# A two-block hybrid network on one core: scan steps, latent norms, angles and the modulated norm placed anew

## The chip, the core and the metric

One core of a Trainium2 chip runs the whole program once. The metric is the device time in microseconds of that core, median of the runs.

## The reference, cut to what matters

256 tokens, width 2048, everything in float32. The first block is an S5 layer (a linear state space with a scan over time, gates z and glu) and a forgetting-attention layer. The second block has two hybrid layers, each with retention and latent attention behind a norm that is modulated by a condition vector:

```
xn = rmsnorm(h, g_pre); u, z = split(xn @ w_in)              # S5 layer
y = s5_ssm(u, ...)                                           # h_t = A h_(t-1) + B u_t, y_t = C h_t + D u_t
y = gelu(y); y = y * sigmoid(y @ w_glu + b_glu) * silu(z); h = h + rmsnorm(y @ w_out, g_post)
kvf = rmsnorm(h, g_kv) @ w_kv                                # keys k, values v, forget gates f
...
mod = silu(c) @ w_mod + b_mod; shift, scale, gate = split(mod, 3)          # hybrid layer, twice
h = rms_norm(x, g_norm) * (1 + scale) + shift
rq, rk, rv, rg, cq, ckv, kr, mg, bg = split(h @ w_in)
rq, rk = rope(rq), rope(rk)                                  # cos and sin of positions * frequencies
q = rms_norm(cq, g_cq) @ w_uq; kv = rms_norm(ckv, g_ckv) @ w_ukv; k_rope = rope(kr)
...
```

## The kernel before

Activations lie transposed, features on the 128 partitions and 256 tokens along the free axis, 16 tiles of 256 columns for the width of 2048. Every weight matrix is streamed from memory in blocks of 128 x 2048 floats, one block per output tile, into four buffers `raw`. For precision each operand is split in two halves that TensorE multiplies at full rate: ScalarE rounds a block to `whi` (L512, `split_hi`), VectorE subtracts it to get `wlo` (L1073, `split_lo`), two buffers of each. TensorE multiplies `whi` by both halves of the activations `xs` (L1893) and `wlo` by the high half (L1895); z and a few others take the form at L1888 and L1890, the value projections v and rv the form at L1854.

Each engine has its own instruction list, written out by hand in the order in which it runs; engines meet only at semaphores. `project(key, ..., side=...)` stands in each list for one matrix: for block j it handles output tile j (TensorE multiplies, ScalarE copies one half of the sum to `acctmp`, L560, VectorE adds the other, L1142), then splits block j + 2, then calls `side(j)`, the place where everything else is hung in. So VectorE's order in block j is: a multiply-add of the modulation stream if the matrix has one (L1101, `modacc`), the sum of tile j, the split of block j + 2, side(j). With `held` the last split of a matrix is left out and issued later by hand. SyncE loads a `raw` buffer again as soon as `w_lo_done` says that its block is split. TensorE may start a tile once the tile two before it has been summed (`acc_summed`).

The places that the change touches:

- z (first block, 16 tiles): `scan_step` runs the S5 scan beside z on VectorE, 62 steps of four instructions (L1267, `s5c` and `ring`); `scanned_by[j]` says how many steps are done after side(j). ScalarE copies the states to `state` in groups of four (`keep_states`, L736), in a ring of twelve. Then TensorE computes the state outputs (`carried`, L2089), which wait for all the states.
- v: `trig_side` on VectorE takes the angles from the positions (`reduce_angle`, L1256 to L1264), seven or eight instructions that each wait for the one before, in blocks 4, 6, 8 and 10; block 13 scales two groups of the next norm (`norm_split`, L1217). The values' tiles are finished only in every fourth block (3, 7, 11, 15), two at a time, and summed at L1134. ScalarE takes the sines in blocks 8 and 12 (L858).
- the modulated norm (`modulate` on ScalarE, L612 and L631; `norm_modulated` on VectorE): four groups of four tiles. VectorE multiplies a group by the reciprocal root (L1267, `stg`), ScalarE applies scale and shift in four instructions (L612), copies the high half (L631), VectorE subtracts for the low half (L1205). The first tile of rq waits for one group after the other.
- the latent norms: cq (512 features) is normalised beside ckv, and ckv beside mg, in one side call each (`latent`): root, reciprocal (L1192), four scalings (L1217), high half (L631), low half (L1205). `mg_side(2)` on VectorE rotates the rope keys.
- `ret_side(0)` on TensorE, beside ga: the wait before the retention scores (L2178), for the last rotation (`rope_done`) and for the centred values (`values_centred`, ScalarE, L547).

## Time and profile before

| | |
|---|---|
| median of 3 runs | 3175.7 us (3175.69 to 3175.76) |
| profiled execution | 3178.53 us |
| its span | 3176.8 us |
| mean granted TensorE clock | 0.986 of full speed |
| TensorE (PE) | busy 95% of the span |
| VectorE (DVE) | 68% |
| ScalarE (ACT) | 48% |
| the 16 DMA engines | mean 203 GB/s |

The span runs from the first to the last instruction of the profiled execution; its own time has 1.7 us more around it. Busy shares are means over stages with different limits. The list of waits gives, for each pair of line and releaser, the idle time of the engine before that line. A matmul counts as busy until its modelled end.

### The profile page before, as it was taken

The page shows a single profiled execution, that of the slowest core. Times are in us where ns is not written, and L with a number is a line of the kernel's source. Part 1 is how long each engine was busy: PE and PEld are TensorE (multiplying, and loading weights), DVE is VectorE, ACT ScalarE, POOL GpSimd, SP SyncE. Part 2 cuts the span into 40 slices and gives each one's busy share as a digit, 9 for nine tenths or more (in the row PEclk, how much of TensorE's full clock was granted, in tenths as well). Part 3 has the DMA queues.
Part 4 walks back from the last instruction along what each step waited for, and adds up shares of the span by engine and source line. Part 5 has one row for each costly group of instructions (what it writes and reads, how often), then busy time and mean ns, then how long its engine had stood idle before and what let it go on. Part 6 is the DMA issues. An engine that isn't in the chain of part 4 may idle for free.

```text
span 3176.8 us, 50173 instructions
## 1 busy us (share of the span) xinstructions
PE 3025.8 (95%) x20326; PEld 2634.6 (83%) x20326; DVE 2154.8 (68%) x2512; ACT 1537.5 (48%) x2007; POOL 108.0 (3%) x206
## 2 busy tenths in 40 slices
PE   6998998999999799999999999989999999999998
PEld 5898887877888687888888888878788888888887
DVE  7688777877865657667765667764755776655565
ACT  5454455334445546345455444453534544554444
POOL 0000000000000000000000000000000000000000
PEclk9999998999999999999999999999999999999999
DMA  5334675776544457656654477645754566445543
GB/s 220 121 108 147 212 257 218 278 257 233 206 166 169 164 200 275 239 189 235 236 215 146 173 283 264 230 182 200 260 191 171 200 234 230 145 174 211 186 176 129
DMA packets 103460, 645.73 MB, mean 203 GB/s; under 512 B 11616, under 2 KB 12640, under 8 KB 40160
## 3 DMA queue, kind: packets, MB, share of 16 engines
q1 hardware_dynamic: 71568, 508.12, 45.1%
q0 software_dynamic: 28528, 105.92, 9.3%
q10 hardware_dynamic: 3168, 28.84, 2.3%
q8 instruction: 152, 2.49, 0.3%
q14 instruction: 44, 0.36, 0.0%
HBM read 628.15 MB, written 14.68 MB: 202 GB/s over the span
## 4 chain that ended last, share of the span: by engine, by line
PE 78%; DVE 12%; ACT 6%; issue 2%; DMA 1%; DVEq 0%; ACTq 0%; POOLq 0%
PE acc L1893 39%; PE acc L1895 19%; PE acc L1854 8%; DVE wlo L1073 4%; PE acc L1888 3%; ACT whi L512 3%; DVE xs L1205 1%; PE acc L1890 1%; DVE s5c L1267 1%; PE bank L2038 1%; DVE w L1267 1%; DVE stg L1726 1%; DVE modacc L1101 1%; PE bank L2233 1%; DMA modw<-in_modstream 1%
## 5 line engine op out<-in xcount | busy, mean ns | idle before, releaser
L1893 PE MATMUL acc<-xs,whi 128*128 128x512 f32 x6192 | 2211.7, 402 | 71.6 <-DVE xs L1205 52.2
L1895 PE MATMUL acc<-xs,wlo 128*128 128x256 f32 x6192 | 1743.0, 281 | 0.0
L1893 PEld LDWEIGHTS acc<-xs,whi 128*128 128x128 f32 x6192 | 1170.6, 189 | 366.7 <-issue 36.4
L1073 DVE TENSOR_TENSOR wlo<-raw,whi 128x2048 fp32r<-128x2048 f32 x451 | 1033.6, 2292 | 505.0 <-ACT whi L512 504.1
L1895 PEld LDWEIGHTS acc<-xs,wlo 128*128 128x128 f32 x6192 | 1177.8, 190 | 1.3 <-issue 0.6
L512 ACT ACTIVATE whi<-raw 128x2048 fp32r<-128x2048 f32 x451 | 860.2, 1907 | 111.9 <-PE acc L1854 105.2
L560 ACT ACTIVATE acctmp<-acc 128x256 f32<-128x256 f32 x387 | 148.0, 383 | 987.6 <-PE acc L1895 976.8
L1142 DVE TENSOR_TENSOR w<-acc,acctmp 128x256 f32<-128x256 f32 (+1 forms) x352 | 152.3, 433 | 328.9 <-ACT acctmp L560 328.2
L1854 PE MATMUL acc<-whi,xs 128*128 128x512 f32 x768 | 242.7, 395 | 11.9 <-DVE w L1134 7.1
L1101 DVE SCALAR_TENSOR_TENSOR modacc<-modw,cact,modacc 128x1024 f32<-128x1024 f32 x180 | 230.2, 1279 | 6.9 <-DMA modw<-in_modstream 6.5
L1854 PEld LDWEIGHTS acc<-whi,xs 128*128 128x128 f32 x768 | 145.7, 190 | 46.7 <-issue 8.3
L491 POOL DMA_DIRECT2D modw<-in_modstream x192 | 101.5, 529 | 2225.7 <-DVE modacc L1098 1254.2
L1854 PE MATMUL acc<-wlo,xs 128*128 128x512 f32 x384 | 151.0, 393 | 0.0
L650 ACT ACTIVATE smx<-smx,stat 128x128 f32<-128x128 f32 x96 | 43.0, 448 | 170.4 <-DVE stat L1293 170.4
L1086 DVE TENSOR_TENSOR wlo<-raw,whi 128x512 fp32r<-128x512 f32 (+1 forms) x96 | 74.7, 780 | 61.3 <-ACT whi L519 60.1
L1888 PE MATMUL acc<-xs,whi 128*128 128x256 f32 x512 | 94.5, 287 | 2.2 <-DVE wlo L1073 2.2
L1854 PEld LDWEIGHTS acc<-wlo,xs 128*128 128x128 f32 x384 | 73.0, 190 | 14.8
L1888 PEld LDWEIGHTS acc<-xs,whi 128*128 128x128 f32 x512 | 81.0, 195 | 2.5 <-DVE wlo L1073 2.4
L1888 PE MATMUL acc<-cqs,whi 128*128 128x256 f32 x384 | 71.5, 288 | 2.5 <-DVE wlo L1086 1.1
L1890 PE MATMUL acc<-xs,wlo 128*128 128x256 f32 x256 | 73.2, 286 | 0.0
L519 ACT ACTIVATE whi<-raw 128x512 fp32r<-128x512 f32 (+1 forms) x96 | 66.7, 695 | 0.2
L1888 PEld LDWEIGHTS acc<-cqs,whi 128*128 128x128 f32 x384 | 59.6, 192 | 4.6 <-DVE wlo L1086 1.9
(304 smaller groups left out, 2313.9 us busy)
## 6 DMA issues: line engine op xcount, KB each, us to landing
raw<-in_wstream SPq DMA_DIRECT2D x479, 1024.0 KB, 4.8
modw<-in_modstream POOLq DMA_DIRECT2D x192, 512.0 KB, 4.6
residual<-h ACTq DMA_DIRECT2D x2, 2048.0 KB, 10.9
ga_gate<-w ACTq DMA_DIRECT2D x2, 2048.0 KB, 10.5
gated_retention<-w ACTq DMA_DIRECT2D x2, 2048.0 KB, 7.9
h<-gated_retention ACTq DMA_DIRECT2D x2, 2048.0 KB, 10.2
h<-residual ACTq DMA_DIRECT2D x2, 2048.0 KB, 9.4
ga_w<-ga_gate ACTq DMA_DIRECT2D x8, 512.0 KB, 10.1
```

What stands on the lines that cost most here:

```text
L491: pool.dma_start(modw[s][:, :], src).then_inc(mod_loaded[s], 16)
L512: act.activation(whi[s % SPL][:, :], raw[slot][:, :], ACT.Copy).then_inc(w_hi_done, 1)
L560: act.activation(acctmp[:, par % 2, :], acc[par % 2][:, T:2 * T], ACT.Copy, scale=FOX_SCALE if key == (None, "q") else 1.0).then_inc(acc_l ...
L1073: dve.tensor_tensor(out=wlo[s % SPL][:, :], in0=raw[s % RAW][:, :], in1=whi[s % SPL][:, :].bitcast(F32), op=ALU.subtract).then_inc(w_lo_do ...
L1086: ins = dve.tensor_tensor(out=wlo[n % SPL][:, c], in0=raw[n % RAW][:, c], in1=whi[n % SPL][:, c].bitcast(F32), op=ALU.subtract)
L1101: dve.scalar_tensor_tensor(out=modacc[:, :], in0=modw[s % 2][:, :], scalar=scale, in1=modacc[:, :], op0=ALU.mult, op1=ALU.add).then_inc(mo ...
L1142: dve.tensor_tensor(out=dest(jt), in0=turn(acc[par % 2][0:rows, 0:T]), in1=turn(acctmp[0:rows, par % 2, :]), op=ALU.add).then_inc(acc_summ ...
L1854: mm = pe.matmul(acc[t % 2][:, :], x_split[:, k0 + k, a, tokens], part_w[:, c], start=(first and k == 0 and part_w is whi[w] and a == 0), ...
L1888: pe.matmul(acc[par % 2][:, 0:T], whi[w][:, c:c + cols], x_split[:, k, a, :], start=(k == 0 and a == 0), stop=False, skip_group_check=True)
L1890: mm = pe.matmul(acc[par % 2][:, 0:T], wlo[w][:, c:c + cols], x_split[:, k, 0, :], start=False, stop=(k == kts - 1), skip_group_check=True)
L1893: pe.matmul(acc[par % 2][0:cols, :], whi[w][:, c:c + cols], x_split[:, k, :, :], start=(k == 0), stop=False, skip_group_check=True)
L1895: mm = pe.matmul(acc[par % 2][0:cols, 0:T], wlo[w][:, c:c + cols], x_split[:, k, 0, :], start=False, stop=(k == kts - 1), skip_group_check ...
```

## The change

- `scanned_by` puts two scan steps fewer into block 4 of z and stays two behind until block 13; block 14 gets five. z's last two weight splits (`held=2`) leave the loop on VectorE and are issued behind the last scan step. VectorE no longer waits for the end of each z tile.
- The two latent norms are cut over two blocks: root and reciprocal in one, scalings and halves in the next. The key rotation moves from mg's block 2 to block 4.
- The angles are computed in `angle_step`, three instructions a block from block 2 to block 12 of v; positions are converted in block 1. The eight scalings of the next norm go two a block into blocks 11 to 14. The second pair of sines moves to block 13.
- In groups 1 and 3 of the modulated norm VectorE multiplies by the modulated scale and the reciprocal root at once (four instructions), ScalarE adds the shift while it writes the high half, and VectorE adds the shift again while it subtracts (four instructions).
- TensorE waits for `values_centred` in block 2 of ga instead of block 0, and for the sums of rv in block 0.

```diff
@@ -121,6 +121,7 @@
 MID_KNOWN = 6
+SHIFT_LATE = (1, 3)
 FOX_FIRST = 3
@@ -424,7 +425,7 @@
-        scanned_by = (4, 12, 20, 28, 36, 37, 38, 39, 42, 45, 48, 51, 54, 57, 60, 62)
+        scanned_by = (4, 12, 20, 28, 34, 35, 36, 37, 40, 43, 46, 49, 52, 55, 60, 62)
@@ -607,6 +608,15 @@
                     act.wait_ge(sem("norm_scaled"), 4 * (name == "pre_l1") + g + 1)
+                    if g in SHIFT_LATE:
+                        act.wait_ge(acc_done, JOBS[(0 if name == "pre_l0" else 1, "rq")][1])
+                        for k in range(4):
+                            i = 4 * g + k
+                            last = act.activation(xs[:, i, 0, :], stg_half(g)[:, k, :], ACT.Identity, bias=mv[:, i:i + 1])
+                            if k == 2:
+                                last.then_inc(x_staged, 1)
+                        last.then_inc(x_hi_done, 1)
+                        continue
                     for k in range(4):
@@ -852,8 +862,8 @@
-                if j in (8, 12):
-                    kind = (j - 8) // 4
+                if j in (8, 13):
+                    kind = (j - 8) // 5
                     act.wait_ge(sem("trig_arg"), kind + 1)
@@ -983,6 +993,7 @@
                         root(f"cq{l}")
+                    if j == 3:
                         act.wait_ge(sem("residual_away"), 16 * (l + 1))
@@ -994,8 +1005,8 @@
                         root(f"ckv{l}")
+                    if j == 2:
                         split_x(f"ckv{l}", lambda g: ckr[:, :, :], cks, 0)
-                    if j == 2:
                         act.wait_ge(acc_summed, JOBS[(l, "mg")][1])
@@ -1122,9 +1133,6 @@
                             lo_piece(*piece, q)
-                        if key == (None, "z"):
-                            dve.wait_ge(acc_done, t + 1)
-                            continue
                         if one_half(key, jt) or key[1] == "rv":
@@ -1144,7 +1152,7 @@
                             link(tt(dest(jt), dest(jt), rstd[0:rows, :], ALU.mult))
-                    if whole and split_ahead(key, j) and not (held and j == JOBS[key][2] - 1):
+                    if whole and split_ahead(key, j) and not (held and isinstance(j, int) and j >= JOBS[key][2] - held):
                         split_lo(j + (b0 + SPL), b0 + s + SPL)
@@ -1230,10 +1238,25 @@
                             dve.wait_ge(x_lo_done, SPLIT_BEFORE[name] + g - 1)
-                        tt(stg_half(g), group(src)(g), bcast(spread_rstd(name), 4), ALU.mult).then_inc(sem("norm_scaled"), 1)
+                        if g in SHIFT_LATE:
+                            for k in range(4):
+                                i = 4 * g + k
+                                ins = dve.scalar_tensor_tensor(out=stg_half(g)[:, k, :], in0=src[:, i, :], scalar=gsc[:, i:i + 1],
+                                                               in1=spread_rstd(name), op0=ALU.mult, op1=ALU.mult)
+                            ins.then_inc(sem("norm_scaled"), 1)
+                        else:
+                            tt(stg_half(g), group(src)(g), bcast(spread_rstd(name), 4), ALU.mult).then_inc(sem("norm_scaled"), 1)
                     if g == 3:
                         split_held((0, "out") if l else (None, "foxout"))
-                    if g >= 1:
+                    if g - 1 in SHIFT_LATE:
+                        dve.wait_ge(x_hi_done, SPLIT_BEFORE[name] + g)
+                        for k in range(4):
+                            i = 4 * (g - 1) + k
+                            ins = dve.scalar_tensor_tensor(out=xs[:, i, 1, :], in0=stg_half(g - 1)[:, k, :],
+                                                           scalar=modv[l][:, i:i + 1], in1=xs[:, i, 0, :].bitcast(F32),
+                                                           op0=ALU.add, op1=ALU.subtract)
+                        ins.then_inc(x_lo_done, 1)
+                    elif g >= 1:
                         split_x(name, stg_half, xs, g - 1)
@@ -1476,7 +1499,9 @@
                     output_power(3, (j - 5,))
-            project((None, "z"), None, side=z_side)
+            project((None, "z"), None, side=z_side, held=2)
+            split_lo(GLU_BLOCK, GLU_BLOCK)
+            split_lo(GLU_BLOCK + 1, GLU_BLOCK + 1)
             dve.wait_ge(sem("c_sigmoid"), 1)
@@ -1582,20 +1607,50 @@
+            def angle_step(n):
+
+                kind, n = divmod(n, 16)
+                quarter, n = (0, n) if n < 8 else (1, n - 7)
+                angle, k, dst = angs[1][:, :], angs[2][:, :], trig[:, kind, 1 - quarter, :]
+                if n == 0:
+                    link(dve.tensor_scalar(angle, angs[0][:, :], invf[:, kind:kind + 1], None, ALU.mult))
+                if n == 1:
+                    link(dve.tensor_scalar(k, angle, 1 / (2 * math.pi), 0.25 * quarter, ALU.mult, ALU.add))
+                if n == 2:
+                    link(dve.tensor_scalar(k, k, MAGIC, None, ALU.add))
+                if n == 3:
+                    link(dve.tensor_scalar(k, k, MAGIC, None, ALU.subtract))
+                if n in (4, 5, 6):
+                    link(dve.scalar_tensor_tensor(out=dst, in0=k, scalar=-(TWO_PI_1, TWO_PI_2, TWO_PI_3)[n - 4],
+                                                  in1=angle if n == 4 else dst, op0=ALU.mult, op1=ALU.add))
+                if n == 7 and quarter:
+                    link(dve.tensor_scalar(dst, dst, math.pi / 2, None, ALU.add))
+                if n == 7 + quarter:
+                    ins = dve.tensor_scalar(dst, dst, PI, -PI, ALU.min, ALU.max)
+                    if quarter:
+                        ins.then_inc(sem("trig_arg"), 1)
+
+            def pre1_tile(i):
+
+                return dve.scalar_tensor_tensor(out=stg_half(i // 4)[:, i % 4, :], in0=h[:, i, :], scalar=vcol("norm_pre1")(i),
+                                                in1=rstd[:, :], op0=ALU.mult, op1=ALU.mult)
+
             def trig_side(j):
-                if j == 3:
+                if j == 1:
                     dve.wait_ge(sem("positions_loaded"), 16)
                     link(dve.tensor_copy(angs[0][:, :], posi[:, :]))
-                if j in (4, 8):
-                    kind = (j - 4) // 4
-                    link(dve.tensor_scalar(angs[1][:, :], angs[0][:, :], invf[:, kind:kind + 1], None, ALU.mult))
-                    link(reduce_angle(trig[:, kind, 1, :], angs[1][:, :], angs[2][:, :], False))
-                if j in (6, 10):
-                    kind = (j - 6) // 4
-                    reduce_angle(trig[:, kind, 0, :], angs[1][:, :], angs[2][:, :], True).then_inc(sem("trig_arg"), 1)
-                if j == 13:
-                    norm_split("pre1", h, vcol("norm_pre1"), stage_only=True)
+                for n in range(3 * (j - 2), 3 * (j - 1)):
+                    if 0 <= n < 32:
+                        angle_step(n)
+                if j in (11, 12):
+                    for i in range(2 * j - 18, 2 * j - 16):
+                        pre1_tile(i)
+                if j in (13, 14):
+                    for i in range(2 * j - 26, 2 * j - 24):
+                        last = pre1_tile(i)
+                    if j == 14:
+                        last.then_inc(x_staged, 2)
             project((None, "v"), lambda j: tile(w2, j), side=trig_side)
@@ -1732,15 +1787,22 @@
                 def latent(n, lat, dst):
-                    rms(f"{n}{l}")
                     norm_split(f"{n}{l}", lat, vcol(f"g_{n}{l}"), staged=lambda g: lat[:, :, :], dst=dst)
-                project((l, "ckv"), lambda j: tile(ckr, j), side=lambda j: latent("cq", cqr, cqs) if j == 2 else None)
+
+                def cq_side(j):
+                    if j == 2:
+                        rms(f"cq{l}")
+                    if j == 3:
+                        latent("cq", cqr, cqs)
+                project((l, "ckv"), lambda j: tile(ckr, j), side=cq_side)
                 project((l, "kr"), lambda j: krope[:, :])
                     if j == 1:
+                        rms(f"ckv{l}")
+                    if j == 2:
                         latent("ckv", ckr, cks)
-                    if j == 2:
+                    if j == 4:
                         link(rope(ROPE_L * l + 8, rtmp[:, 0:1, :], krope[:, :].rearrange("p (a t) -> p a t", a=1), 1, 1))
@@ -2194,6 +2256,8 @@
                         pe.wait_ge(rope_done, ROPE_L * l + 8)
+                        pe.wait_ge(acc_summed, JOBS[(l, "ga")][1])
+                    if j == 2:
                         pe.wait_ge(sem("values_centred"), RET_H * (l + 1))
```

## Rows read from the trace of the kernel before

**Rows 1.** Page, first section: busy time (share of the span) and instructions.

```profile
PE 3025.8 (95%) x20326; PEld 2634.6 (83%) x20326; DVE 2154.8 (68%) x2512; ACT 1537.5 (48%) x2007; POOL 108.0 (3%) x206
```

**Rows 2.** Waits of TensorE: line <- releaser: us in total, times, longest.

```profile
PE acc L1893 <- DVE xs L1205: 52.2, 18, 8.7
...
PE acc L1854 <- DVE w L1134: 7.1, 3, 3.2
```

**Rows 3.** Timeline, TensorE: start, us, instruction, [idle before <- releaser], four stretches.

```profile
244.36 0.51 PE L1888 MATMUL acc<-xs,whi 128*128 128x256 f32 x2 [2.19 <-DVE wlo L1073]
...
305.35 4.92 PE L2089 MATMUL bank<-vall,state 64*64 64x64 f32 x87 [7.42 <-ACT state L736]
...
1273.10 0.70 PE L2178 MATMUL bank<-w 128*128 128x256 f32 x2 [1.52 <-DVE w L1267]
...
1523.74 0.50 PE L1893 MATMUL acc<-xs,whi 128*128 128x512 f32 x1 [1.61 <-DVE wlo L1073]
...
1550.27 0.50 PE L1893 MATMUL acc<-xs,whi 128*128 128x512 f32 x1 [2.14 <-DVE wlo L1073]
```

**Rows 4.** Windows: length, PE, PEld, DVE, ACT, POOL busy, PEclk, DMA share, GB/s.

```profile
244.40:248.70 4.30, 4.30 (x24) 4.30 (x25) 4.27 (x6) 0.93 (x1) 0.00 (x0) 0.61 0.74 244
248.70:251.80 3.10, 3.10 (x27) 3.10 (x27) 3.07 (x6) 0.00 (x0) 0.00 (x0) 0.99 0.35 42
305.30:310.20 4.90, 4.85 (x91) 4.88 (x93) 0.00 (x0) 0.00 (x0) 0.00 (x0) 0.50 0.33 135
310.20:316.00 5.80, 5.80 (x203) 5.80 (x199) 2.14 (x4) 1.99 (x4) 0.00 (x0) 1.00 0.01 3
657.00:659.60 2.60, 2.04 (x10) 1.36 (x9) 2.49 (x4) 0.52 (x2) 0.00 (x0) 1.00 0.65 197
685.20:689.00 3.80, 3.80 (x10) 3.06 (x11) 3.58 (x3) 0.00 (x0) 0.53 (x1) 0.56 0.88 259
1523.70:1529.50 5.80, 5.76 (x33) 5.01 (x33) 3.28 (x3) 0.65 (x1) 0.53 (x1) 1.00 0.74 256
```

**Rows 5.** Timeline, VectorE beside z: splits (wlo) and the scan's last instruction.

```profile
242.02 2.28 DVE L1073 TENSOR_TENSOR wlo<-raw,whi 128x2048 fp32r<-128x2048 f32 x1
...
254.21 2.29 DVE L1073 TENSOR_TENSOR wlo<-raw,whi 128x2048 fp32r<-128x2048 f32 x1 [1.04 <-ACT whi L512]
...
294.51 2.29 DVE L1073 TENSOR_TENSOR wlo<-raw,whi 128x2048 fp32r<-128x2048 f32 x1
...
300.26 2.29 DVE L1073 TENSOR_TENSOR wlo<-raw,whi 128x2048 fp32r<-128x2048 f32 x1
...
304.41 0.29 DVE L1267 TENSOR_TENSOR ring<-s5c 128x128 f32<-128x128 f32 x1
```

**Rows 6.** Timeline, VectorE beside v, blocks 6 and 7.

```profile
680.42 0.29 DVE L1256 TENSOR_SCALAR angs<-angs 128x256 f32<-128x256 f32 x1
...
681.40 0.43 DVE L1259 SCALAR_TENSOR_TENSOR trig<-angs,angs 128x256 f32<-128x256 f32 x1
...
683.32 1.28 DVE L1101 SCALAR_TENSOR_TENSOR modacc<-modw,cact,modacc 128x1024 f32<-128x1024 f32 x1
684.51 0.87 DVE L1134 TENSOR_SCALAR w<-acc,ms 128x256 f32<-128x256 f32 x2
```

**Rows 7.** Timeline, VectorE and ScalarE in the latent norms of the first layer.

```profile
1514.67 1.75 DVE L1192 RECIPROCAL rstd<-rstd 128x256 f32<-128x256 f32 x1 [0.48 <-ACT rstd L620]
1516.46 1.67 DVE L1217 SCALAR_TENSOR_TENSOR cqr<-cqr,vec,rstd 128x256 f32<-128x256 f32 x4
1519.32 1.23 DVE L1205 TENSOR_TENSOR cqs<-cqr,cqs 128x1024 fp32r<-128x1024 f32 x1 [1.19 <-ACT cqs L631]
...
1544.17 1.06 ACT L631 ACTIVATE cks<-ckr 128x1024 fp32r<-128x1024 f32 x1 [3.53 <-DVE ckr L1217]
```

**Rows 8.** Timeline, VectorE in the modulated norm of the first layer.

```profile
1078.64 1.22 DVE L1267 TENSOR_TENSOR stg<-h,rstd 128x1024 f32<-128x1024 f32 x1
1080.49 1.23 DVE L1205 TENSOR_TENSOR xs<-stg,xs 128x1024 fp32r<-128x1024 f32 x1 [0.64 <-ACT xs L631]
...
1086.73 1.23 DVE L1205 TENSOR_TENSOR xs<-stg,xs 128x1024 fp32r<-128x1024 f32 x1 [0.42 <-ACT xs L631]
```

## The prediction

> **What bounds the kernel now.** I read the page's first section, then the list of TensorE's waits, then the rows just behind each wait. TensorE is busy for 95% of the span [rows 1], so an edit on another engine is worth something only where TensorE stands still, or runs at the lower of its two clocks after standing still. Of the waits the change can reach [rows 2], the reader is to see four places. (a) The scan beside z: TensorE stands 2.19 us before the eighth tile of z, and 7.42 us between z and the state outputs [rows 3]. (b) The value projection v: three waits for VectorE's sum of a tile, 7.1 us together, the longest 3.2 [rows 2]; in the trace they are 0.6, 3.25 and 3.25. (c) The latent norms: 1.61 and 2.14 us before two weight splits [rows 3], and the same pair 1050.6 us later in the second layer, so four waits. (d) The modulated norm at the head of each layer, most of the 52.2 us behind L1205 [rows 2]. For the fifth edit (e) the wait is 1.52 us at L2178 [rows 3], also twice.
>
> **(a) Scan ahead of the splits.** VectorE has no pause here: one split and three scan steps fill 5.75 us, 294.51 to 300.26 [rows 5]; less 2.29 for the split, a step is 1.15 us. The new table puts six steps instead of eight behind block 4, and keeps two steps of lag from there to block 13. So the split that TensorE waited for at 244.36 begins 2 x 1.15 = 2.3 us before 242.02 and is done at 242.0, when TensorE's tile before it ends (244.36 - 2.19 = 242.17). The 2.19 us go. So does the slow stretch behind them: 24 matmuls took 4.3 us at a granted clock of 0.61, where the next 27 took 3.1 us at 0.99 [rows 4]; 4.3 - 24 x 0.115 = 1.5 us. TensorE is 3.7 to 3.9 us earlier from there on. VectorE is earlier by 2.3 us plus the 1.04 it used to wait for ScalarE at 254.21 [rows 5], 3.4 in all, so each later split, which used to be done about 1.0 us before TensorE wanted it (288.7 + 2.3 against 292.0), keeps some 0.5 us. That is thin, but the period of 5.75 doesn't exceed z's 48 matmuls x 0.12 = 5.76.
> The tail: the scan's last step ended at 304.41 + 0.29 = 304.70 [rows 5]. Now, from 294.51 - 3.4 = 291.1, come five steps (5.8) and two (2.3) with no split between: 299.15. The states' copy and TensorE follow as before, at 299.8 instead of 305.35: **-5.5 us**. This includes the 3.8 above, since the later start is what counts. The wait for the end of each z tile that VectorE loses is implied by ScalarE's half of the split; the ring of states keeps its copies (step 57 wants twelve groups, copied beside block 12). The two splits moved behind the scan (299.2 to 303.8) are covered by the state outputs: VectorE idled from 304.8 to 311.6 before, and 306.1 answers to that end now; without this cover they would cost 4.6. SyncE's load of the fifth glu block waits for the first of them, 5 us later than now, against a use after 345: nothing. The state outputs start at the lower clock, 91 matmuls in 4.9 us against 203 in the next 5.8 [rows 4]. The idle time before them shrinks from 7.4 to some 5.8 us, so how long the low clock lasts is not given by a row: at most 91 x (53.8 - 28.6 ns) = 2.3 us gained, and as much lost if it lasted twice as long. I take 0.6, near no change: **-0.6 us**.
>
> **(b) Angles spread, first norm groups in four pieces.** Eight operations in one block (680.42 to 683.32, 2.90 us) made VectorE late for the multiply-add of the modulation (1.19) and with it for the sum that frees TensorE's accumulator [rows 6]. A TENSOR_SCALAR with its wait takes 0.33, a fused one 0.46. Before the sum of block 7 now stand two fused and one plain, 1.25: the wait of 3.25 becomes 1.6. Before block 11's, three plain ones, 0.98: 3.25 becomes 1.33. Before block 3's, three at 1.04 where none was: 0.58 becomes 1.62. Together 1.65 + 1.92 - 1.04 = 2.5 us. After each long wait TensorE ran at a clock of 0.56 to 0.58: 10 matmuls in 3.8 us against 10 in about 2.1 [rows 4], 1.5 us, twice: 3.0. The wait of 1.61 us at 1523.74 is followed by a granted clock of 1.00 [rows 4], so I take the whole 3.0; nothing to 3.0 is the range. Pieces of the norm (0.42 a piece, four of them 1.67 [rows 7]) leave block 13 with 0.8 instead of 3.3 us and bring the last multiply-add 0.3 us forward. In every other block VectorE has 2.2 + 1.2 + 1.1 to 2.2 against 5.44 of TensorE, so these steps are hidden; that cover is 0.9 us and more. Positions are used two blocks earlier, at 652.4, 12 us after they landed: nothing. **-5.8 us**.
>
> **(c) Latent norms in two blocks.** Before, reciprocal (1.75), four scalings (1.67), ScalarE's half (1.06) and the difference (1.22) all stood before the next split [rows 7]. With the scalings a block later, VectorE splits mg's first block at 1518.9 to 1521.1; TensorE starts it at 1522.0 instead of 1523.74, -1.75. What is late next is ScalarE: it waits for the scalings (1522.75), makes its half, and only then copies kr and splits the next block, which VectorE finishes at 1528.3, 0.6 us after TensorE wants it. Net -1.15. For ckv: the split is done at 1547.1, before it is wanted at 1548.1, so -2.14; but ScalarE waits for the scalings until 1548.8, then half (1.06), swap (0.85), copy, split, and VectorE is done at 1555.1 where TensorE wants it at 1553.7: +1.4. With the queue's 0.15, net -0.9. The keys' rotation, two blocks later, falls into a block with 0.8 us to spare. Two layers: **-4.1 us**; if the new waits are absent -7.5, if they are half as long again -2.
>
> **(d) Modulated scale by VectorE in groups 1 and 3.** ScalarE paced this pipeline: VectorE waited 0.64 and 0.42 us for it [rows 8]. ScalarE loses two halves of 1.06. VectorE's product of 1.22 becomes four fused operations, 1.67, and its difference likewise. Between the first difference and the last it gains three times 0.45 = 1.35 and loses 1.06 of waiting; the split held for the layer stands among them and moves too. End of the last difference +0.35, and the last quarter of TensorE's first tile with it. Two layers: **+0.7 us**; -0.5 to +1.5.
>
> **(e) The values' wait.** TensorE's wait of 1.52 us ends with VectorE's L1267 [rows 3], the last rotation, whose wait stays where it is. The centring was over 6 us before. The added wait is for sums already made. **0**, at most 0.2 either way.
>
> **The sum** is -5.5 - 0.6 - 5.8 - 4.1 + 0.7 = -15.3 us on the profiled execution's 3178.5 (span 3176.8); the runs' median lies 2.8 us below that execution, and the same difference gives 3175.7 - 15.3 = **3160.4**.
>
> **Rule against row.** The rows show the clock at its lower level, 1.2 instead of 2.4 GHz, after TensorE stood for 2.19 and 3.25 us [rows 3, 4]. The Trainium skill, page "TensorE: Matmul & The Clock Gate", section "HAM oscillation — how this bites in real kernels", counts only idle gaps longer than each of these as a danger. By that rule none of the three slow stretches should be there, and removing the gaps would return only their own length: 4.5 us less, 3164.9. The row differs and decides.
>
> **The rivals.** (1) *The clock stays as expensive*: the three remaining waits in v (1.3 to 1.6 us) are each followed by the lower clock. For it: after 2.19 us it fell. Against: after 1.61 it didn't [rows 4]. Then v gives -1.3 at best and the whole -10.8: 3164.9. Chance 0.10. (2) *New waits take the places*: VectorE misses z's splits, whose margin is 0.5 us, and the two latent waits are as long as those removed. Then (a) gives -3, (c) 0, the sum -8.1: 3167.6. Chance 0.07. (3) *The norm gives more*: DMA and clock fall better behind the earlier start (waits of 2.2 to 2.9 us at the heads of later stages sometimes carry the low clock, 1.5 us each), two or three of them: 3156.5. Chance 0.13. (4) *Within 0.2%*: TensorE is earlier, but the modulation's stream makes the q stage and the s5out stage wait as long again, so that only half arrives: 3170. Chance 0.05. (5) *Slower*: steps spread one to three a block cost what their waits cost, not their length. It decides once a step in v takes over 0.3 us more than the 0.33 to 0.46 of the row, since then every block overruns 5.44; at 1.3 us more a step ten blocks pay 3.0 each, +30 us, giving 3190. Against it, the same operations stand back to back with the same waits in rows 6. Chance 0.03. (6) *An edit doesn't do what it says* (e, or d): both are near 0 in the sum already.
>
> **How the numbers follow.** My forecast 3160.4 has 0.62. The range of 8 in 10 must take in rivals 1 and 3 and the bounds of (b), (c) and the clock in (a): 3155.0 to 3167.0. About 0.2% (6.3 us) is what a measurement can tell from no change: below 3169.4 is faster, 0.92; 0.05 the same; 0.03 slower.
>
> **What the new profile would show.** No wait of L1888 in z; state outputs at 299.8 +- 0.7; two splits behind the last scan step. In v, waits near 1.6, 1.6 and 1.3 and no clock below 1.00. In both layers, waits at mg's blocks 1 and 5 instead of 0 and 4. VectorE without pause in the modulated norm. L2178's wait unchanged. It would be wrong if z's splits are late, or if the latents' waits only move.

## The result, and the profile after

The changed kernel takes 3159.7 us, the median of 9 executions (3153.2 to 3169.5). Nine executions of the kernel before, on the same chip, have a median of 3173.9 (3163.1 to 3182.1). The ratio is 0.995, 95% interval 0.9938 to 0.9962: of 3173.9 us that is 15.9 us less (12.1 to 19.7). The prediction was 15.3 less, 3160.4. The profiled execution of the changed kernel took 3157.37 us, with a span of 3155.7 and a mean granted clock of 0.987, against 3176.8 and 0.986.

Those two traces differ by 21 us, more than the medians do. Single executions of one kernel scatter by about 10 us on either side, and the 21 us lie outside the interval of the medians, so the 5 us surplus is not put down to the change; part of the work below is to find where it sits.

The page of the changed kernel, first section, answers to [rows 1] (busy time, share of the span, instructions):

```profile
PE 3017.1 (96%) x20326; PEld 2627.1 (83%) x20326; DVE 2157.7 (68%) x2536; ACT 1532.7 (49%) x2003; POOL 108.5 (3%) x206
```

Its waits of TensorE, answering to [rows 2] (line <- releaser: us in total, times, longest). L1955 is now what L1893 was, L1916 what L1854 was:

```profile
PE acc L1955 <- DVE xs L1213: 49.6, 18, 8.7
PE acc L1955 <- DVE wlo L1084: 15.7, 23, 2.5
...
PE bank L2151 <- ACT state L746: 5.3, 1, 5.3
...
PE acc L1916 <- DVE w L1142: 5.0, 3, 1.8
```

The waits of v are 5.0 us instead of 7.1, the wait of z before its eighth tile is gone (no line L1950 with a weight split of 2.2 us), and the one before the state outputs is 5.3 instead of 7.4. The timeline of TensorE in the changed kernel shows each in its place, answering to [rows 3]:

```profile
298.36 1.94 PE L2151 MATMUL bank<-vall,state 64*64 64x64 f32 x31 [5.28 <-ACT state L746]
...
653.15 0.47 PE L1916 MATMUL acc<-whi,xs 128*128 128x512 f32 x1 [1.62 <-DVE w L1142]
677.02 0.47 PE L1916 MATMUL acc<-whi,xs 128*128 128x512 f32 x1 [1.83 <-DVE w L1142]
700.60 0.47 PE L1916 MATMUL acc<-whi,xs 128*128 128x512 f32 x1 [1.56 <-DVE w L1142]
...
1260.66 0.70 PE L2240 MATMUL bank<-w 128*128 128x256 f32 x2 [1.52 <-DVE w L1290]
...
1516.27 0.50 PE L1955 MATMUL acc<-xs,whi 128*128 128x512 f32 x1 [0.65 <-DVE wlo L1084]
1542.16 0.49 PE L1955 MATMUL acc<-xs,whi 128*128 128x512 f32 x1 [1.39 <-DVE wlo L1084]
```

Windows of the changed kernel, answering to [rows 4] (the clock is the number before the DMA share):

```profile
298.30:304.40 6.10, 6.04 (x114) 6.07 (x116) 3.89 (x3) 0.00 (x0) 0.00 (x0) 0.50 0.58 192
304.40:310.20 5.80, 5.80 (x185) 5.73 (x183) 2.81 (x4) 2.53 (x4) 0.00 (x0) 1.00 0.41 168
...
677.00:684.00 7.00, 6.98 (x31) 5.82 (x32) 4.61 (x6) 1.75 (x2) 1.06 (x2) 1.00 0.81 291
```

VectorE at the scan's end: its last step, and the two splits that now stand behind it, answering to [rows 5]:

```profile
297.41 0.29 DVE L1290 TENSOR_TENSOR ring<-s5c 128x128 f32<-128x128 f32 x1
297.62 4.49 DVE L1084 TENSOR_TENSOR wlo<-raw,whi 128x2048 fp32r<-128x2048 f32 x2
```

And VectorE in the modulated norm of the first layer, answering to [rows 8]:

```profile
1059.16 1.23 DVE L1290 TENSOR_TENSOR stg<-h,rstd 128x1024 f32<-128x1024 f32 x1
1060.30 1.67 DVE L1244 SCALAR_TENSOR_TENSOR stg<-h,gsc,rstd 128x256 f32<-128x256 f32 x4
1063.67 1.23 DVE L1213 TENSOR_TENSOR xs<-stg,xs 128x1024 fp32r<-128x1024 f32 x1 [1.71 <-ACT xs L641]
...
1066.08 1.67 DVE L1255 SCALAR_TENSOR_TENSOR xs<-stg,modv,xs 128x256 fp32r<-128x256 f32 x4
...
1072.70 1.67 DVE L1255 SCALAR_TENSOR_TENSOR xs<-stg,modv,xs 128x256 fp32r<-128x256 f32 x4
1077.90 0.42 DVE L1150 TENSOR_TENSOR w<-acc,acctmp 128x256 f32 x1 [3.54 <-ACT acctmp L561]
```

The pauses of 0.64 and 0.42 between the differences are gone, as predicted; the wait before the first difference, 2.15 us before, is still 1.71. The last row is the first sum of rq: it comes 3.53 us after the last difference, where it came 2.39 after it before.

### The profile page after: what moved, and what is told of

Same layout as the page of the kernel before. It is cut to its first block, busy times and chain, and to the rows that moved or that the text cites. A ratio compares the mean times of both kernels' runs of the same rounds, so it can differ in the third digit from the quotient of the medians.

```text
span 3155.7 us, 50181 instructions
## 1 busy us (share of the span) xinstructions
PE 3017.1 (96%) x20326; PEld 2627.1 (83%) x20326; DVE 2157.7 (68%) x2536; ACT 1532.7 (49%) x2003; POOL 108.5 (3%) x206
## 4 chain that ended last, share of the span: by engine, by line
PE 80%; DVE 11%; ACT 6%; issue 2%; DMA 0%; DVEq 0%; ACTq 0%; POOLq 0%
PE acc L1955 39%; PE acc L1957 20%; PE acc L1916 8%; DVE wlo L1084 4%; PE acc L1950 3%; ACT whi L513 3%; DVE xs L1213 2%; PE acc L1952 2%; PE bank L2100 1%; DVE w L1290 1%; DVE stg L1781 1%; PE bank L2297 1%; PE bank L2112 1%; PE bank L2151 1%; PE bank L2298 1%
## 5 line engine op out<-in xcount | busy, mean ns | idle before, releaser
L1955 PE MATMUL acc<-xs,whi 128*128 128x512 f32 x6192 | 2208.0, 401 | 65.6 <-DVE xs L1213 49.6
L1955 PEld LDWEIGHTS acc<-xs,whi 128*128 128x128 f32 x6192 | 1168.4, 189 | 361.1 <-issue 36.6
L1916 PE MATMUL acc<-whi,xs 128*128 128x512 f32 x768 | 239.6, 391 | 9.8 <-DVE w L1142 5.0
L1916 PEld LDWEIGHTS acc<-whi,xs 128*128 128x128 f32 x768 | 144.2, 188 | 43.4 <-DVE wlo L1084 7.4
L1916 PE MATMUL acc<-wlo,xs 128*128 128x512 f32 x384 | 149.5, 389 | 0.0
L1950 PE MATMUL acc<-xs,whi 128*128 128x256 f32 x512 | 92.9, 284 | 0.0
L1916 PEld LDWEIGHTS acc<-wlo,xs 128*128 128x128 f32 x384 | 72.1, 188 | 14.7
L1950 PEld LDWEIGHTS acc<-xs,whi 128*128 128x128 f32 x512 | 79.7, 192 | 0.1
L1950 PE MATMUL acc<-cqs,whi 128*128 128x256 f32 x384 | 71.4, 287 | 2.6 <-DVE wlo L1097 1.1
L1950 PEld LDWEIGHTS acc<-cqs,whi 128*128 128x128 f32 x384 | 59.5, 191 | 4.6 <-DVE wlo L1097 1.9
```

The source lines that it names most:

```text
L1916: mm = pe.matmul(acc[t % 2][:, :], x_split[:, k0 + k, a, tokens], part_w[:, c], start=(first and k == 0 and part_w is whi[w] and a == 0), ...
L1950: pe.matmul(acc[par % 2][:, 0:T], whi[w][:, c:c + cols], x_split[:, k, a, :], start=(k == 0 and a == 0), stop=False, skip_group_check=True)
L1955: pe.matmul(acc[par % 2][0:cols, :], whi[w][:, c:c + cols], x_split[:, k, :, :], start=(k == 0), stop=False, skip_group_check=True)
```

## The experiments

**How they are compared.** Every kernel has the same 20326 matmuls in the same order. So the start of the same matmul can be looked up in two traces, and the difference over a stretch is what the stretch gained. The limits are times of the kernel before; positive is us gained against its trace. z is 186 to 300, v 640 to 737, the latents 1500 to 1560 and 2550 to 2611, the modulated norms 1040 to 1090 and 2110 to 2145.

| kernel | z | v | latents 1 | latents 2 | mod. norm 1 | mod. norm 2 | all the rest | whole trace |
|---|---|---|---|---|---|---|---|---|
| changed | 6.02 | 6.05 | 1.78 | 1.48 | -2.80 | -0.58 | 9.08 | 21.03 |
| (a) alone | 5.97 | 0.36 | -0.01 | -0.02 | -0.21 | -1.19 | 5.88 | 10.78 |
| (b) alone | -0.13 | 4.47 | -1.34 | -0.22 | -3.20 | -0.70 | 4.14 | 3.02 |
| (c) alone | 1.50 | 0.30 | 1.78 | 1.45 | -0.12 | -1.35 | 15.53 | 19.09 |
| (d) alone | -0.02 | -1.17 | -1.54 | -0.02 | -3.88 | -1.06 | 2.65 | -5.04 |
| (e) alone | 1.42 | 0.28 | -1.39 | -1.41 | -0.27 | -0.61 | 10.94 | 8.96 |
| all three follow-ups | 5.97 | 9.34 | 4.25 | 4.46 | -0.57 | 1.55 | 8.38 | 33.38 |

The column of the rest is the warning: no part touches what is in it, and it runs from 2.7 to 15.5 here, and from -1.9 to 15.5 over all the kernels of this document.

### One part at a time

Four kernels: the kernel before with the hunks of one part of the diff each, as the prediction names them. Of (a), beside the lines that let `project` hold two splits:

```diff
-        scanned_by = (4, 12, 20, 28, 36, 37, 38, 39, 42, 45, 48, 51, 54, 57, 60, 62)
+        scanned_by = (4, 12, 20, 28, 34, 35, 36, 37, 40, 43, 46, 49, 52, 55, 60, 62)
...
-                        if key == (None, "z"):
-                            dve.wait_ge(acc_done, t + 1)
-                            continue
...
-            project((None, "z"), None, side=z_side)
+            project((None, "z"), None, side=z_side, held=2)
+            split_lo(GLU_BLOCK, GLU_BLOCK)
+            split_lo(GLU_BLOCK + 1, GLU_BLOCK + 1)
```

> Only the scan's new table and z's two held splits on VectorE; the rest is the kernel before. My theory (the prediction's part a): the 2.19 us wait in z and its slow stretch go, the state outputs start 5.5 us earlier than in the kernel before, and about 5 us of time go in all, ratio 0.9982 to 0.9986. Rival, new waits take the places: TensorE waits for z's splits in several tiles and the state outputs start 3 us earlier or less, ratio 0.999 and more.

Measured: 3169.5 us against 3174.4, ratio 0.9985 (0.9972 to 0.9997), which is in the range expected. In the trace z gained 5.97.

(b), the `angle_step` and `trig_side` hunks and ScalarE's sines in block 13:

> Only the angles three steps a block and the norm's pieces in v. My theory: v's waits are 1.6, 1.6 to 1.8 and 1.3 to 1.6 us instead of 0.6, 3.25, 3.25, the granted clock stays at its upper level through v, and v is 5.8 us shorter, half of it from the clock. Rival, the clock stays as expensive: each of the three waits is followed by a stretch at the lower level of 1.5 us cost, and v is only 1.3 us shorter. Ratio 0.9980 by the first, 0.9996 by the second.

Measured: 3174.9 against 3174.4, ratio 0.9999 (0.9985 to 1.0013). The waits are those of the changed kernel, but v gained 4.47 instead of 6.05. The timeline of TensorE, and two windows behind the second wait:

```profile
683.50 0.47 PE L1884 MATMUL acc<-whi,xs 128*128 128x512 f32 x1 [1.83 <-DVE w L1134]
```

```profile
683.60:687.80 4.20, 4.20 (x12) 3.30 (x13) 3.86 (x6) 0.38 (x1) 0.53 (x1) 0.59 0.88 269
687.80:692.00 4.20, 4.20 (x20) 3.46 (x20) 0.62 (x1) 1.18 (x1) 0.53 (x1) 1.00 0.85 343
```

The same wait of 1.83 us that left the clock at 1.00 in the changed kernel is followed here by 0.59: 12 matmuls where the next 4.2 us hold 20. The 1.6 us between 6.05 and 4.47 are this stretch: up to the matmul of 685.2 us the two gained the same (0.61 and 0.63), at 691 us 2.23 and 0.66. For the whole kernel the run is inconclusive: its interval reaches from 4.8 us less to 4.1 more, which just holds the local gain.

(c), `cq_side`, `latent`, the two `split_x` on ScalarE and the key rotation:

> Only the latent norms over two blocks and the key rotation two blocks later. My theory: in each layer TensorE waits 0.6 us before mg's second block and 1.4 us before its sixth instead of 1.6 before the first and 2.1 before the fifth, 2.0 us a layer, 4.1 in all, ratio 0.9987. Rival, the waits only move: their sum stays 3.7 us a layer, ratio 1.000.

Measured: 3165.6 against 3174.4, ratio 0.9981 (0.9968 to 0.9994). The waits of 0.65 and 1.39 are there, at 1520.42 and 1546.32; the latents gained 1.78 and 1.45, 3.2 in all. The interval of the ratio is 1.9 to 10.2 us less.

(d), `modulate` and `norm_modulated`:

> Only the modulated norm with VectorE's scale in two groups. My theory: VectorE is the bound, and from the first difference (L1205 of before) to the end of the last it takes 10.6 to 10.9 us as before (10.58 in the first layer, 10.87 in the second), so the time is within 0.7 us, ratio 1.0000 to 1.0002. Rival, it costs the clock: TensorE runs at the lower level behind its second wait in that tile, as in the changed kernel, because the change makes it so; then the first tile of rq ends 1.2 us later in each layer, 2.4 in all, ratio 1.0008. If the lower clock there doesn't show in this run, it isn't this edit that brings it.

Measured: 3175.4 against 3174.4, ratio 0.9998 (0.9987 to 1.001). Its trace does show the lower clock in the first tile of rq; whether the edit brings it is taken up below, with all traces.

The four ratios add up to 0.37%, 11.7 us, against 15.9 (12.1 to 19.7) for the whole. With intervals of 4 us each way on every part that is agreement, no more.

### Which half of (a) does it

Two kernels: the held splits with the old table, and the new table without the held splits.

```diff
-                        if key == (None, "z"):
-                            dve.wait_ge(acc_done, t + 1)
-                            continue
...
+            project((None, "z"), None, side=z_side, held=2)
+            split_lo(GLU_BLOCK, GLU_BLOCK)
+            split_lo(GLU_BLOCK + 1, GLU_BLOCK + 1)
```

VectorE's wait for the end of each z tile goes with this half. In the kernel before VectorE stood for no such end between 195 and 304 us, so the splits are what this kernel tests.

> The kernel before with one half of part (a): z's last two weight splits are issued behind the last scan step, the table of scan steps stays as it was. My theory (two effects that add: the table starts z's eighth tile earlier, the held splits end the scan earlier): the wait of 2.19 us before z's eighth tile stays, the last scan step ends two splits (4.6 us) earlier, and the state outputs start near 301.0 us, 4.4 us earlier than before. The rival (the table alone does it, because the splits only hide behind ScalarE's copies of the states): state outputs at 304 to 305 us, at most 1 us gained.

```diff
+        scanned_by = (4, 12, 20, 28, 34, 35, 36, 37, 40, 43, 46, 49, 52, 55, 60, 62)
```

> The other half of part (a): the new table of scan steps alone; the last two splits stay in the loop. My theory: no wait before z's eighth tile and no low clock behind it, so TensorE is 3.8 us earlier inside z, but stands that much longer at z's end, since the scan still ends behind both splits: state outputs near 304.4 us, about 1 us gained. The rival: the state outputs come as much earlier as z does, near 301.5 us.

Their whole times, 3174.4 and 3172.3 against 3173.1, are single executions and say nothing. All traces have a first product of the output powers early in z (L2050 before), and the times of the table are counted from its start. That is 193.88 us in the kernel before:

```profile
193.88 1.30 PE L2050 MATMUL bank<-w,k 128*128 128x256 f32 x7 [0.71 <-ACT k L729]
```

| kernel | idle before z's eighth tile, clock behind it | scan's last step ends | state outputs start |
|---|---|---|---|
| before | 2.19, 0.61 | +110.82 | +111.47 |
| (e) alone, z as before | 2.15, 1.00 | +109.30 | +109.95 |
| new table alone | none | +109.19 | +109.84 |
| held splits alone | 2.07, 1.00 | +104.79 | +106.18 |
| (a) alone | none | +104.81 | +105.47 |
| changed | none | +104.79 | +105.45 |

The kernel with (e) alone has z as it was, and it makes the table readable. Windows of 4.3 us just behind that wait, of the kernel with (e) alone (for the kernel before it is the first of [rows 4]):

```profile
243.10:247.40 4.30, 4.24 (x35) 4.24 (x36) 4.27 (x7) 1.04 (x1) 0.00 (x0) 1.00 0.62 242
```

35 matmuls instead of 24 behind a wait of the same length. So the low clock there is no fixed price: of six kernels that keep this wait, it followed in three (waits of 2.19, 2.20, 2.21) and did not in three (2.07, 2.15, 2.16). Where it didn't, the scan ended 1.5 us earlier with nothing changed. VectorE shows the way: its wait of 1.04 us for ScalarE before a split in z ([rows 5]) stands in the three traces with the low clock there and in none of the other eleven. From the trace without it the held splits give 109.30 - 104.79 = 4.5 us, two splits, and the new table 0.1 at the scan's end. What the table adds is at the state outputs: with the splits held but the old table they start 1.39 us after the scan's last step, released by ScalarE's copy of the states, with both 0.66 us after it. These are 0.7 us: at the state outputs the held splits alone are worth 109.95 - 106.18 = 3.8 us, with the table 4.5. Why the copy is late with the old table was not looked into. Otherwise the table only takes away the wait that may bring the low clock. The theory of two effects that add was half right: the held splits gave what was expected of them (within 0.7 us), and the 3.8 us earlier tiles inside z gave nothing, as expected of the table alone.

### Without (d), and (e) alone

> The changed kernel without part (d), so with the modulated norm as it was. If (d) is worth next to nothing, as the trace of it alone says: VectorE's stretch from the first difference to the last one takes 10.6 us in layer 1 and 10.9 in layer 2, with its pauses of 0.64 and 0.42 us back, and the first tile of rq is summed as soon after the last difference as the clock allows, 2.4 to 3.7 us; the rest of the program is as in the changed kernel, span 3155 to 3160 us. The rival, that (d) brings 1.5 to 3 us where the modulated norm runs (the changed kernel is 2.8 us shorter between 1040 and 1090 us): here that stretch is as long as in the kernel before.

Measured: 3158.0 us, one execution, beside 3157.4 for the profiled one of the changed kernel; the two pauses are back (0.63 and 0.41 us). The expectation has a sign wrong: between 1040 and 1090 us the changed kernel is 2.8 us longer than the kernel before, not shorter. Here that stretch is 0.4 us longer. (b) alone, which has no (d) either, is 3.2 us longer there, so this pair decides nothing. (e) alone:

```diff
                         pe.wait_ge(rope_done, ROPE_L * l + 8)
+                        pe.wait_ge(acc_summed, JOBS[(l, "ga")][1])
+                    if j == 2:
                         pe.wait_ge(sem("values_centred"), RET_H * (l + 1))
```

> The kernel before with part (e) alone: TensorE waits for the centred values in ga's third block and for the sums of rv in the first. Predicted nothing: the wait before the retention scores stays 1.52 us in both layers, and stays named after VectorE's last rotation. It is also as good as a second trace of the kernel before. If the low clock falls at other waits from one execution to the next, the stretches around 957 to 1090, 1840 and 2110 to 2140 us differ from the trace of before by 1.5 to 4 us though nothing there is changed; if the clock is set by the program alone, they agree within 0.3 us.

Measured: 3169.4 us against 3173.1, single executions. The wait stays, here in both layers:

```profile
1264.27 0.70 PE L2178 MATMUL bank<-w 128*128 128x256 f32 x2 [1.51 <-DVE w L1267]
...
2313.32 0.70 PE L2178 MATMUL bank<-w 128*128 128x256 f32 x2 [1.52 <-DVE w L1267]
```

So (e) is worth nothing, and this trace, 9.0 us shorter than that of the kernel before, shows what two executions of as good as one program differ by: 1.42 in z, 1.4 the other way in each layer's latents (the low clock behind another spot), and the remainder in stretches that nobody touched. Of the stretches that the expectation named none differs as much as it said: 957 to 1090 gained 0.4 us in all, 1820 to 1860 gained 0.1, 2110 to 2140 lost 0.3. The differences of its size lie elsewhere (2.1 us at 1890 to 1920, beside those in z and in the latents). They decide against a clock set by the program alone. One pair of rows shows it best, the wait before mg's fifth block in the first layer, 2.14 us in both traces. The kernel before:

```profile
1550.27 0.50 PE L1893 MATMUL acc<-xs,whi 128*128 128x512 f32 x1 [2.14 <-DVE wlo L1073]
...
1550.30:1554.60 4.30, 4.30 (x24) 3.74 (x25) 4.20 (x8) 2.28 (x3) 0.53 (x1) 1.00 0.91 316
```

and the one with (e) alone:

```profile
1541.71 0.52 PE L1893 MATMUL acc<-xs,whi 128*128 128x512 f32 x1 [2.14 <-DVE wlo L1073]
...
1541.70:1546.00 4.30, 4.29 (x15) 3.71 (x16) 4.20 (x8) 2.28 (x3) 0.53 (x1) 0.60 0.86 301
```

24 matmuls against 15 behind a wait of one length, so the length of the wait does not decide it.

For the modulated norm I take two lengths: from the start of VectorE's first multiplication by the reciprocal root to the end of its last difference, and to the start of the first sum of rq.

| kernel | layer 1: last difference | first sum | layer 2: last difference | first sum |
|---|---|---|---|---|
| before | 15.09 | 17.48 | 15.38 | 17.77 |
| changed without (d) | 15.09 | 17.48 | 15.39 | 19.03 |
| changed | 15.21 | 18.74 | 15.19 | 18.92 |
| (d) alone | 15.21 | 19.83 | 15.19 | 18.83 |
| follow-up: latents in three blocks, with (d) | 15.20 | 17.60 | 15.18 | 18.77 |
| follow-up: held split late, with (d) | 13.74 | 16.12 | 13.71 | 16.11 |

VectorE's own time is the same to 0.2 us with and without (d). What varies is the 2.4, 3.6 or 4.6 us behind it: TensorE has one more piece of the norm to multiply, at the full or at the low clock, after standing 1.7 to 3.2 us for it. In layer 2 the longer end came in 11 of 12 traces with this wait, whether (d) was in or not. In layer 1 it came in 1 of 8 without (d) and in 3 of 4 with it. That hints that (d) costs a share of 1.1 to 2.2 us in layer 1, but with so few traces it stays open; the ratio of (d) alone bounds it, between 3.2 us more and 4.1 less for all of (d).

### Follow-ups: taking the remaining waits away

All three start from the changed kernel. First, the latent norms over three blocks:

```diff
                     if j == 3:
-                        latent("cq", cqr, cqs)
+                        scale_latent("cq", cqr)
...
+                    if j == 0:
+                        split_x(f"cq{l}", lambda g: cqr[:, :, :], cqs, 0)
+                    if j == 3:
+                        scale_latent("ckv", ckr)
+                    if j == 5:
+                        split_x(f"ckv{l}", lambda g: ckr[:, :, :], cks, 0)
```

> The changed kernel with the latent norms cut over three blocks: reciprocal, scalings, and halves and difference each in a block of its own, and the key rotation one block on. My theory of the two new waits (0.65 us before mg's second block and 1.39 before its sixth: ScalarE must wait for the scalings before it makes its half, and so copies and splits late): ScalarE finds the scalings done a block before, both waits go, and nothing of the same size comes in their place, so 2.0 us a layer more than the changed kernel, 4.1 in all, in the stretches 1500 to 1560 us and its like 1045 us later. The rival (the waits come from VectorE's own work, which is 0.4 to 0.7 us too much for two blocks however it is cut): the waits stay within 0.5 us of 2.04 in sum, or move one block on.

Measured: 3153.9 us, one execution. The waits before mg's second and sixth block are gone in both layers, and nothing stands in their place. One window over both spots, the changed kernel and this one:

```profile
1515.00:1545.00 30.00, 27.96 (x156) 23.90 (x155) 23.86 (x24) 16.45 (x17) 2.12 (x4) 1.00 0.66 226
```

```profile
1515.00:1545.00 30.00, 30.00 (x173) 26.36 (x172) 24.33 (x23) 16.42 (x17) 2.64 (x5) 1.00 0.72 249
```

TensorE is busy for 30.00 of 30 us instead of 27.96: the 2.04 us. The stretches gained 4.84 and 4.04 against the kernel before, so 3.1 and 2.6 more than the changed kernel. Of these 2.4 a layer fall at the two waits: each cost TensorE 0.16 to 0.18 us more than its length in the changed kernel. The others are spread over stretches without any wait (the two paces of the last section). Who was late is read from ScalarE, in the changed kernel:

```profile
1535.64 1.06 ACT L641 ACTIVATE cks<-ckr 128x1024 fp32r<-128x1024 f32 x1 [3.94 <-DVE ckr L1225]
```

and in this one:

```profile
1541.83 1.05 ACT L641 ACTIVATE cks<-ckr 128x1024 fp32r<-128x1024 f32 x1
```

It stood 3.94 us for the scalings, with the copy of a tile and the next weight block queued behind; now they are done when it comes.

Second, the angle steps four a block in eight blocks, with no step in the blocks just ahead of the sums of the values' tiles (2, 6, 10):

```diff
-                for n in range(3 * (j - 2), 3 * (j - 1)):
-                    if 0 <= n < 32:
+                beside = (3, 4, 5, 7, 8, 9, 11, 12)
+                if j in beside:
+                    for n in range(4 * beside.index(j), 4 * beside.index(j) + 4):
                         angle_step(n)
```

> The changed kernel with the angle steps placed four a block in blocks 3, 4, 5, 7, 8, 9, 11 and 12 of v, so that none but the modulation's multiply-add stands right before a sum of a tile of values... except that block's own work. My theory: what TensorE waits for in v is the length of the steps between a tile's end and its sum, each 0.33 to 0.46 us; with none there, the waits of 1.62, 1.83 and 1.57 us go back to about 0.6 each, which is 3.0 us less for v than in the changed kernel, and no low clock. The rival (the waits are the multiply-add's and would be the same without the steps): they stay above 1.3 us, and v takes as long.

Measured: 3155.5 us, one execution. All three waits are at 0.57 to 0.58, and v gained 9.33 instead of 6.05, 3.3 us more:

```profile
652.82 0.47 PE L1917 MATMUL acc<-whi,xs 128*128 128x512 f32 x1 [0.57 <-DVE w L1142]
675.42 0.47 PE L1917 MATMUL acc<-whi,xs 128*128 128x512 f32 x1 [0.58 <-DVE w L1142]
698.05 0.47 PE L1917 MATMUL acc<-whi,xs 128*128 128x512 f32 x1 [0.58 <-DVE w L1142]
```

Third, the held weight split behind the last difference:

```diff
-                    if g == 3:
-                        split_held((0, "out") if l else (None, "foxout"))
...
+                split_held((0, "out") if l else (None, "foxout"))
```

> The changed kernel with the held weight split (2.1 us of VectorE) issued behind the last difference of the modulated norm instead of between the differences. VectorE has no pause there in the changed kernel, so its own work is what sets the last difference: my theory is that the time from the first multiplication to the end of the last difference shrinks from 15.2 us by 1.2 to 2.1 us in each layer (ScalarE's halves bound it from below), and that TensorE's first tile of rq is summed as much earlier, less or more 1.2 us by the clock. The rival (ScalarE or the clock sets the end): it shrinks by less than 0.5 us, or TensorE waits for the split behind it instead, and rq's first tiles are done at the same time.

Measured: 3164.3 us, one execution, whose trace lost 3.2 us before 186 and 3.5 between 300 and 440, where nothing differs; the norm is read from the table above. VectorE is done 1.5 us earlier, and both layers' first sums come 2.4 us behind the last difference: the wait before the tile's last piece is now 1.2 and 1.0 us, and the low clock followed it in neither layer of this kernel, nor of the one with all three. TensorE of this kernel:

```profile
1075.81 0.50 PE L1954 MATMUL acc<-xs,whi 128*128 128x512 f32 x1 [1.18 <-DVE xs L1213]
1078.03 0.49 PE L1954 MATMUL acc<-xs,whi 128*128 128x512 f32 x1 [0.54 <-DVE xs L1253]
1080.23 0.50 PE L1954 MATMUL acc<-xs,whi 128*128 128x512 f32 x1 [0.54 <-DVE wlo L1084]
```

The last row is the split that was moved: TensorE waits 0.54 us for it, so the rival was right about a part. The second sum of rq comes 22.6 us after the first multiplication, in the changed kernel 24.4, in the kernel with the latents in three blocks (no low clock in layer 1) 23.3: 0.7 us by the move itself and 1.1 by the clock.

Then all three together:

> All three at once on the changed kernel: latent norms over three blocks (4 us), angle steps off the sums (3 us), held split late (2 us). If the waits that I name are each the last thing late in their stage, the sum is 9 us less than the changed kernel: about 3151 us, a ratio to the kernel before of 0.992. If the waits only move, it stays at 3158 to 3160, a ratio of 0.995.

Measured: **3145.4 us** (3141.1 to 3148.6, 6 executions) against 3172.7 (11 executions), ratio **0.9915** (0.9901 to 0.9929), and the interval does not touch that of the changed kernel. By the rows it should be 13.1 us below the changed kernel: 3.3 in v, 5.4 in the latents (8.71 - 3.26), and in the modulated norms 2.6 + 2.8 to the first sum (its own are 16.13 and 16.11) less twice the 0.54 of the new wait. The medians differ by 14.2 us, the ratios by 0.35%, 11.1 us. The expectation had said 9: it gave the latents 4 and the late split 2, and left out what the lower clock costs in the modulated norm. Its waits of TensorE:

```profile
PE acc L1964 <- DVE xs L1215: 47.1, 18, 8.7
...
PE acc L1964 <- DVE wlo L1086: 11.1, 20, 1.5
```

## Why the prediction was right

The sum of 15.3 us stands against 15.9 measured (12.1 to 19.7), and the range and the side were right. Its terms were not all so.

**(a), predicted -5.5 and -0.6.** The state outputs came 6.02 us earlier on the trace's own count, so -5.5 was 0.5 short. In the prediction's own sum the 2.3 us of the table come back as two more steps in block 14, so its -5.5 is two splits, 4.6, and VectorE's 1.04 us of waiting for ScalarE. The first is right: the runs give 4.5, and the table moves the scan's end by 0.1 us. The second is no fixed price: it comes with the low clock behind the wait of 2.19, which followed in three of six traces, and together they hold the scan back 1.5 us. So over executions (a) is worth some 5.3 us, not 6.0: 4.5 plus half of 1.5. The low clock in the state outputs, where 0.6 was to be gained, went the other way: it lasted from 298.3 to 304.4, 6.0 us of the work instead of 4.9, and by the matmul that started at 316 us the gain of 6.02 is 5.49, so 0.5 lost. In the text both ends of this term had been kept, 2.3 gained and 2.3 lost.

**(b), predicted -5.8; the trace 6.05.** The waits were foretold as 1.62, 1.6 and 1.33, and are 1.62, 1.83 and 1.56. The steps before the sums of blocks 7 and 11 took the 1.25 and 0.98 us of the prediction (from 673.95 to 675.20, and from 697.79 to 698.77). What was off is the base that they stand on: the prediction took 2.90 us of steps off a wait of 3.25, which leaves 0.35, but with no step there the wait is 0.58, as the second follow-up shows. 0.58 + 1.25 is 1.83 and 0.58 + 0.98 is 1.56: of the 2.90 in the kernel before 0.23 had been hidden. The waits therefore gave 2.07 us and not 2.5. Other terms made up for it: behind each of the two long waits 1.6 us of clock came back (3.2, not 3.0; the prediction's own rows, 3.8 against 2.1, say 1.7), and ahead of the second and third wait TensorE was 0.23 us earlier each time. The 0.3 us of the last multiply-add was not kept: 0.34 us appears at the matmul of 737 us and is given back by that of 745, so v is worth 5.71 in this trace. Nor was the cover of the other blocks 0.9 us and more, as its own upper figure, 2.2 + 1.2 + 2.2, is over 5.44; yet no wait appeared there. The clock of 1.00 in all of v came in the changed kernel and in three others with this wait of 1.83, and not in the kernel with (b) alone. So rival 1 (the clock as expensive as before) is true in 1 of 5 traces, for one of the three waits. Seen over executions (b) is worth 5.7 less 0.3, that is 5.4.

**(c), predicted -4.1; 3.26 in the trace.** The new waits of 0.65 and 1.39 us are within 0.05 of the 0.6 and 1.4 foretold, and ScalarE is the one that is late, as the follow-up shows. TensorE did reach mg's first block 1.78 us earlier (1.75 foretold). What was too small is the price of the new waits: the gain fell from 1.98 to 1.17 us at the one of 0.65, and from 3.37 to 1.80 at the one of 1.39, so 0.8 and 1.6 for 0.6 and 1.4; and the net "queue's 0.15" didn't come. In sum that is what the waits alone give, (1.61 + 2.14) - (0.65 + 1.39) = 1.71 a layer, 3.4 in all. In the first layer 1.0 us more seems gained between 1560 and 1620, but the kernel with (e) alone gained the same 1.03 there: it is no effect of (c). The trace of the kernel before was a lucky one for this term, though. It has no low clock behind its four waits, while of the 14 such waits of 1.9 us and more (before mg's fifth block, seven traces without (c)) five were followed by it, at 1.3 to 1.6 us each; of the 10 that (c) leaves there, 1.39 to 1.61 us long, none was. Between the means of the seven traces without and the five with the norms in two blocks (c) is worth 2.3 us in the first layer and 1.9 in the second, 4.3 in all. So -4.1 is near the mark over executions, by a price that the prediction had not counted.

**(d), predicted +0.7; not distinguishable from 0 in VectorE's own time** (+0.12 and -0.19, so -0.1). VectorE without pause between the differences is right. What the prediction did not weigh is the wait before the tile's last piece, and which clock follows it.

**(e), predicted 0; 0.**

So the terms by the runs are -5.3, +0.5, -5.4, -4.3 and -0.1, that is -14.6 us and the part of (d) that is open; the measured interval holds it. That 15.3 lies so near 15.9 is in part luck: the single terms were off by up to 1.1 us, both ways. The 21 us between the two traces consist of 12.0 in the six named stretches and 9.1 elsewhere, where the other traces differ from that of the kernel before by -1.9 to 15.5, whatever is changed in them. The profiled execution of the kernel before was a long one: 3178.5, 4.6 above the median of its nine. The prediction's allowance of 2.8 us from that execution to the median was in the right direction.

**The rule weighed in the prediction.** It would have every low-clock stretch behind a gap of 2.2 and 3.25 us absent; the rows had them. Over 14 traces the picture is finer than either. Behind v's waits of 3.2 us the clock fell in 13 of 14 cases, behind z's waits of 2.07 to 2.21 in 3 of 6, behind the latents' waits of 1.93 to 2.15 in 5 of 14, behind v's wait of 1.83 in 1 of 5, behind v's waits of 1.56 to 1.62 in none of 10. The exception among the first is the second wait of the kernel with (a) alone, whose windows behind the first and the second are:

```profile
677.10:681.10 4.00, 3.97 (x9) 3.14 (x10) 3.67 (x3) 0.00 (x0) 0.53 (x1) 0.50 0.87 264
705.50:709.50 4.00, 4.00 (x18) 3.33 (x19) 3.64 (x3) 0.00 (x0) 0.53 (x1) 1.00 0.70 223
```

The Trainium skill (page "TensorE: Matmul & The Clock Gate", section "HAM oscillation — how this bites in real kernels") counts only longer idle gaps as a danger; for gaps of this length these traces contradict it, most clearly for 3.2 us. The time does too: 3164.9 would be 10.8 us less, and the measured interval begins at 12.1.

## What to carry to other kernels

Where a serial chain on one engine (here the scan) ends a stage, move out of it whatever the next stage doesn't need yet, and count just that: starting its neighbours earlier gave nothing. When an operation is cut out of a block, ask which engine waits for its result in the middle of its own list: ScalarE standing 3.9 us for four scalings cost TensorE 1.4, and one more block between producer and consumer took it away. And before a single trace is believed for a few microseconds, compare it with a second trace of the same program, stretch by stretch.

## What was not expected of the hardware

**The low clock behind a wait of about 2 us is a matter of the execution.** In two programs that are alike up to that place the same wait in z (2.19 and 2.15) was followed once by 0.61 and once by 1.00, and the wait of 2.14 in the latents once by 1.00 and once by 0.60. A term of 1.5 us for it should be entered with a share, not as a whole, and a trace in which it is absent does not show that the wait is cheap.

**TensorE has two paces at a granted clock of 1.00.** In the first fifteen blocks or so of each layer, without any wait, 72 us hold 410 matmuls in one trace and 418 in another. Windows of the kernel before and of the changed one at the same place of the second layer:

```profile
2150.00:2222.00 72.00, 72.00 (x410) 62.41 (x409) 34.54 (x26) 27.82 (x26) 0.00 (x0) 1.00 0.53 183
```

```profile
2130.00:2202.00 72.00, 72.00 (x418) 62.97 (x417) 35.34 (x26) 28.43 (x26) 0.00 (x0) 1.00 0.53 190
```

The same 408 matmuls from there on take 72.08 us in the kernel before and 70.72 in the changed one. Over the 14 traces this length has these two values and nothing between them, seven times each. That is 1.4 us over this stretch, in favour of the change and not its doing: the kernels with one part alone have it in four of five cases, that with (e) alone has it in the first layer instead, and none of the five kernels built on the changed one has it here. Its cause isn't known; no run took it apart.
